# The low part of the weights made by an accumulating DMA instead of a GpSimd subtraction, from the ninth piece on

## The reference

```python
proj = jnp.einsum('bsd,dp->bsp', nx, w_in[l])
...
h = h + jnp.einsum('bsm,md->bsd', mixed, w_out[l])
...
a = jnp.square(jax.nn.relu(jnp.einsum('bsd,df->bsf', nm, w_ff1[l])))
h = h + jnp.einsum('bsf,fd->bsd', a, w_ff2[l])
...
ffn = (jax.nn.silu(hn @ w_gate) * (hn @ w_up)) @ w_down
```

## Time and profile before

| | |
|---|---|
| median of 3 runs | 1548.32 us (1547.88 to 1549.98) |
| the profiled execution: time | 1547.88 us |
| its span | 1546.5 us |
| busy: PE, DVE, ACT, POOL | 94%, 53%, 42%, 36% |
| mean granted TensorE clock | 0.966 of full speed |
| HBM read | 126.93 MB |

### The profile page before, as it was taken

How to read it: one execution, slowest core, us unless ns; L and a number is a source line. 1 busy time by engine, 2 the same in 40 slices (tenths; PEclk the granted TensorE clock), 3 DMA queues, 4 the chain that set the end, 5 groups by cost and what they waited for, 6 DMA issues and landing times.

```text
span 1546.5 us, 17691 instructions
## 1 busy us (share of the span) xinstructions
PE 1449.0 (94%) x6886; PEld 1155.5 (75%) x6886; DVE 824.0 (53%) x1177; ACT 642.1 (42%) x1048; POOL 550.8 (36%) x230
## 2 busy tenths in 40 slices
PE   6989999899999999978988989999899989998998
PEld 4877766688888888856766767787688768876886
DVE  4063466731222313666499889884656642662462
ACT  4353345442322324443466566555344422441340
POOL 3432121344343434333222222223344444444441
PEclk9998899999999999999999999999999999999999
DMA  5321220222222323212211112226232222222321
GB/s 197 117 91 43 66 89 28 82 82 96 96 96 95 98 93 99 92 55 69 68 56 55 55 55 82 81 97 204 83 96 82 96 82 95 95 82 87 104 71 66
DMA packets 41400, 134.39 MB, mean 87 GB/s; under 512 B 4739, under 2 KB 4755, under 8 KB 41189
## 3 DMA queue, kind: packets, MB, share of 16 engines
q1 hardware_dynamic: 40452, 131.67, 26.1%
q10 hardware_dynamic: 864, 1.60, 0.3%
HBM read 126.93 MB, written 6.32 MB: 86 GB/s over the span
## 4 chain that ended last, share of the span: by engine, by line
PE 56%; DVE 27%; ACT 10%; issue 6%; DMA 1%; POOL 0%; DVEq 0%; ACTq 0%; POOLq 0%
PE bank L397 17%; PE bank L399 16%; PE bank L401 16%; DVE ft L1570 4%; DVE ft L1568 3%; ACT WH L689 2%; DVE eb L1306 2%; DVE eb L1302 1%; PE bank L507 1%; DVE ft L1577 1%; ACT AH L980 1%; DVE ft L1563 1%; ACT ft L650 1%; ACT ft L640 1%; ACT ft L638 1%
## 5 line engine op out<-in xcount | busy, mean ns | idle before, releaser
L1629 POOL TENSOR_TENSOR WL<-RAW,WH 128x1024 fp32r<-128x1024 f32 (+2 forms) x225 | 548.3, 2445 | 976.5 <-ACT WH L689 976.1
L397 PE MATMUL bank<-NH,WH 128*128 128x512 f32 x1152 | 475.6, 413 | 12.2 <-ACT NH L670 7.2
L399 PE MATMUL bank<-NL,WH 128*128 128x512 f32 x1152 | 458.3, 398 | 12.7 <-DVE NL L1244 7.7
L401 PE MATMUL bank<-NH,WL 128*128 128x512 f32 x1152 | 456.9, 397 | 0.2 <-POOL WL L1629 0.2
L689 ACT ACTIVATE WH<-RAW 128x1024 fp32r<-128x1024 f32 (+2 forms) x227 | 234.3, 1036 | 298.9 <-PE bank L401 290.2
L397 PEld LDWEIGHTS bank<-NH,WH 128*128 128x128 f32 x1152 | 221.1, 192 | 81.2 <-issue 30.8
L399 PEld LDWEIGHTS bank<-NL,WH 128*128 128x128 f32 x1152 | 221.2, 192 | 63.2 <-DVE NL L1244 9.7
L401 PEld LDWEIGHTS bank<-NH,WL 128*128 128x128 f32 x1152 | 221.0, 192 | 47.9 <-POOL WL L1629 0.6
L397 PE MATMUL bank<-AH,WH 128*128 128x512 f32 x432 | 173.6, 402 | 16.1 <-ACT AH L980 15.7
L1332 DVE TENSOR_TENSOR hT<-hT,bank 128x512 f32<-128x512 f32 x80 | 54.9, 686 | 232.2 <-PE bank L401 232.1
L399 PE MATMUL bank<-AL,WH 128*128 128x512 f32 x432 | 173.1, 401 | 0.0
(11 more groups left out here) (268 smaller groups left out, 1671.2 us busy)
## 6 DMA issues: line engine op xcount, KB each, us to landing
RAW<-in_w_in SPq DMA_DIRECT2D x64, 512.0 KB, 3.8
RAW<-in_w_ff SPq DMA_DIRECT2D x64, 512.0 KB, 3.7
RAW<-in_w_gu SPq DMA_DIRECT2D x44, 512.0 KB, 3.7
RAW<-in_w_down SPq DMA_DIRECT2D x20, 512.0 KB, 3.7
RAW<-in_w_out SPq DMA_DIRECT2D x16, 512.0 KB, 3.8
gates<-hs SPq DMA_DIRECT2D x16, 256.0 KB, 3.3
gw<-gates SPq DMA_DIRECT2D x16, 256.0 KB, 5.9
RAW<-in_w_branch SPq DMA_DIRECT2D x8, 512.0 KB, 3.9
```

The lines of the kernel that those rows point to most:

```text
L397: e.matmul(o, a[0], a[1], start=(k == 0), stop=False)
L399: e.matmul(o, b[0], b[1], start=False, stop=False)
L401: mm = e.matmul(o, c[0], c[1], start=False, stop=(k == t.kt - 1))
L1629: e.tensor_tensor(WL[p % HL][:, 0:n], RAW[p % RAWS][:, 0:n], WH[p % HL][:, 0:n].bitcast(F32), ALU.subtract).then_inc(*pool.sig("low", p))
```

## The change

From the piece with number ADDED = 8 on (219 of 227 pieces), WL isn't subtracted by GpSimd any more. ACT writes the negated high part into WL (a second ACT copy with scale -1), and a DMA that GpSimd issues reads the piece of weights from HBM a second time and adds it into WL, so that WL = W - WH. RAW is now free as soon as WH is made. The negation stands at `split_time(p) + 1.5`, the DMA at `split_time(p) + 3.0`. Each of the five slots has a semaphore of its own for the DMA's end.

```diff
+        ADDED = 8
+
         def low(p):
-            return ("low_first" if p < 2 else "low", p)
+            return ("low_first" if p < 2 else "low" if p < ADDED else f"low_added{p % HL}", p)
...
+        def low_time(p):
+            return split_time(p) + (3.0 if p >= ADDED else 0.05)
...
+            def negated():
+                for p, (u, k, m) in enumerate(plan.pieces):
+                    if p >= ADDED:
+                        yield split_time(p) + 1.5
+                        n = m * plan.units[u][4]
+                        act.wait_ge(("high", p))
+                        e.activation(WL[p % HL][:, 0:n], WH[p % HL][:, 0:n].bitcast(F32), ACT.Copy,
+                                     scale=-1.0).then_inc(*act.sig("high_negated", p))
...
-                    yield split_time(p) + 0.05
-                    n = m * plan.units[u][4]
+                    yield low_time(p)
+                    st, name, i, kt, cols, k0 = plan.units[u]
+                    n = m * cols
+                    if p >= ADDED:
+                        src = A[name] if i is None else A[name][i]
+                        pool.wait_ge(("high_negated", p))
+                        e.dma_start(WL[p % HL][:, 0:n], src[:, k * cols:(k + m) * cols],
+                                    accum_op=ALU.add).then_inc(*pool.sig(f"low_added{p % HL}", p, by=16))
+                        continue
...
-                        sp.wait_ge(low(p - RAWS))
+                        sp.wait_ge(low(p - RAWS) if p - RAWS < ADDED else ("high", p - RAWS))
```

More of the change, by code:

```diff
@@ L981, in swiglu @@
                 return [up(t) if t.i % 2 else gate(t) for t in plan.stage["gu", g]]
-            streams = [prologue(), splits(), root("attn", 14.0), columns("attn", 30.0)]
+            streams = [prologue(), splits(), negated(), root("attn", 14.0), columns("attn", 30.0)]
             streams += [natural("vG", vG, "attn"), natural("vD", vD, "attn")]
```

## The result

Four runs of the changed kernel took 1452.33 to 1453.41 us, median **1452.95 us**. The kernel before, in four runs, took 1549.15 us in the median. The profiled execution, 1452.93 us, has a span of 1451.6 us, 94.9 us less than before.

The account below looks back on a forecast made before the run. PE, busy 94%, was taken as at its peak in f1 and f2, with DVE stopped by POOL's subtraction mattering elsewhere. From 1547.88 us, -18 - 13 - 5 = -36 gave 1512 us; range 1482 to 1645, the forecast's own 1482 to 1544.

Parts of the forecast that it names:

- The rival that the change does nothing: DVE's stops have another cause than POOL's subtraction; gains are lost and negations make it some 1557 us; chance 0.02.
- (c): From 77 to 309 us: 7.5 us of DVE stops in the chain go, negations cost 2.5; net gain 5 us.
- (b): Stick and HGRN2, 735 to 1044 us: 20 us of DVE's excess comes through, negations cost 7; net gain 13 us.
- qS, kS and wo2: Two projections for the stick-breaking attention, ahead of 735 us, and a product behind HGRN2 and the gates: 0 us.
- (a): Handovers from gu to dn: PE's waits for AH, 15.7 us, go, with some lower clock behind them; gain 18 us.
- f1, f2 and the middle of gu: Stretches where PE is at its peak, so nothing off PE can shorten them: 0 us.
- The share of a fifth: In stick and HGRN2, a fifth of 34 us of negations on ACT counted as on the path: 7 us.
- The rival that ACT becomes the bound: Every negation of (b) and (c) on the path: 1562 us; chance 0.10, half of it within no change.
- Two passes: Each added DMA takes 3.2 us of all 16 DMA engines; with a load 4.8 us per piece against PE's 5.52.
- 16.5 of cover: Slot A's time from release to first use, 16.5 us; WL was forecast there after 9 to 12 us.
- the rival of late issues: GpSimd's DMA issues wait for DVE, 0.7 us, at most 2.7; with landing above 9 us, 1644 us; chance 0.03.
- The heavy DMA rivals: DMA engines become the bound: 1634 us at three passes, 1848 at four; chance 0.14 up to three, 0.14 beyond.

Follow-up runs that it names:

- the first two experiments: Changed kernel with GpSimd also subtracting each piece in place in RAW: 1558.54 us; that kernel with three memsets in place of the subtraction: 1461.73 us.
- the copy experiment: Changed kernel in which SP also copies every piece from the ninth on from HBM to a spare place in HBM: 1461.53 us.

## Why the prediction was right in direction and short in size

**The mechanism: right.** DVE's stops beside GpSimd's subtraction were named as what the change takes away, and the first two experiments show it. The rival that the change does nothing falls. The stops were read a little too narrowly: besides operations on two tensors in SBUF, some with one input stood still too, as this line of the kernel before shows (ns min/median/max):

```profile
L629 DVE TENSOR_SCALAR sq<-sq x5: 426/430/2451, 30.9 to 1164.3; 128x512 f32<-128x512 f32 x5
```

What failed is the sum. It left out three quarters of DVE's stops in (c), a third of those in (b) and all those in qS, kS and wo2, and it took PE's busy time as fixed.

**(a), 18 us: right, a little small.** The three handovers gave 23.3. The timeline of the first handover (start us, us, engine, line) answers to the earlier trace rows:

```profile
1172.76 0.61 ACT L657 ACTIVATE ft<-ft 128x512 f32<-128x512 f32 x1
...
1173.41 0.69 DVE L1584 TENSOR_TENSOR ft<-ft,rs 128x512 f32<-128x512 f32 x1 [2.07 <-ACT ft L657]
...
1174.14 0.69 DVE L1586 TENSOR_TENSOR ft<-ft,ft 128x512 f32<-128x512 f32 x1
1174.93 0.69 DVE L1593 TENSOR_TENSOR ft<-bank,ft 128x512 f32<-128x512 f32 x1
...
1175.66 0.63 ACT L996 ACTIVATE AH<-ft 128x512 fp32r<-128x512 f32 x1
```

AH's copy begins as the multiplication with the up tile ends. It begins 2.3 and ends 3.0 us after that tile's last matmul (1173.3 us), where about two and a half were forecast, and PE waits for nothing. Short was what comes on top of the waits, counted at 4 us: it is 7.6 (23.3 less the waits of 15.7). The three handovers gave 9.5, 7.8 and 6.1 us.

**f1, f2 and the middle of gu, 0 us: right** to a tenth of a microsecond. This is what a stretch at PE's full rate looks like in advance, and counting matmuls told it rightly.

**(c), 5 us, against 26.3: the step that failed most.** Only the stops at three places of the chain that ended last were priced, 7.5 us. DVE's busy time in the stretch fell by 30 us, some 2 of them because the later stretch holds three operations fewer. A chain shows one path; a stop beside it, once the path is shortened, can be the next one to hold PE up. And the stretch had a granted clock of 0.93, which wasn't priced at all. Two parts of it, columns as in the earlier trace rows, in the kernel before:

```profile
93.00:136.00 43.00, 38.86 (x167) 28.91 (x166) 23.65 (x32) 16.64 (x30) 11.29 (x5) 0.84 0.14 49
165.00:206.00 41.00, 37.88 (x253) 33.74 (x253) 15.60 (x22) 14.31 (x28) 10.10 (x4) 0.88 0.22 71
```

and about the same work in the changed kernel:

```profile
93.00:126.00 33.00, 32.35 (x164) 24.46 (x163) 18.41 (x32) 20.48 (x35) 3.78 (x5) 1.00 0.59 133
153.00:187.00 34.00, 34.00 (x259) 31.14 (x258) 12.68 (x23) 19.03 (x32) 3.46 (x4) 1.00 0.61 148
```

In the first, 167 matmuls keep PE busy for 38.9 us at 0.84, and 164 for 32.4 us at 1.00: of the 10 us gained 6.5 are busy time, and only the rest are waits. In the second PE was idle for 3.1 of 41 us, yet 7 are gained.

**(b), 13 us, against 28.5 from vS to gs: failed in the same way.** The stops were summed over groups that a reader could pick out and "smaller groups", 30 us; DVE's busy time fell by 46. The granted clock of 0.96 was again not priced, and the sum was then cut from 30 to 20 because PE was busy for 281 of 309 us. That cut was wrong in kind: a PE that is busy at the lower clock isn't at its peak either. The low end of the range doesn't follow from these terms: 19.7 us in (a), 30 in (b) and 7.5 in (c) off 1547.88, with no negation on the path, make 1491, not 1482; the measured time lies under both.

**qS, kS and wo2, 0 us, against 12.3.** They weren't looked at. They lie at the edges of the stretches that were, and DVE's busy time in them fell by 20 us.

The common fault of these steps is that PE's busy time, 37.7 us of the gain, was taken as fixed work. The clock was priced only behind the two longest waits.

**The negations: 9.5 us predicted on the path, 15 to 16 measured.** The share of a fifth was a guess at the middle; the place on ACT turned out to be worth nearly 5 us of it, or 14 against it. The rival that ACT becomes the bound has its mechanism, but not its size. (With half of the negations on the path that rival comes to 1532 by its own terms, 29.5 us in place of 9.5, and not to 1537.)

**The added DMA.** Two passes, 3.2 us, were taken for a piece; 45.9% of 1451.6 us over 219 pieces are 3.04, against 1.57 for a plain load by the prediction's own reckoning (27.1% of 1451.6 us for 131.67 MB, 0.524 MB a piece). The Trainium skill, in Collectives: The Full Stack ("The bandwidth ceiling"), gives half the rate of a plain copy for a reduce-scatter, whose addition in the DMA needs two reads on one ring. That is stated for a transfer between cores; the ratio of 1.94 here agrees with it. The landing was underestimated, 8.6 us against 5.3 to 7:

```profile
RAW<-in_w_ff SPq DMA_DIRECT2D x64, 512.0 KB, 6.0
WL<-in_w_ff POOLq DMA_DIRECT2D x64, 512.0 KB, 8.6
```
```profile
L1648 POOL DMA_DIRECT2D WL<-in_w_ff x64: 862/862/883, 252.9 to 607.0; - x64
L1648 POOL DMA_DIRECT2D WL<-in_w_in x62: 862/862/1569, 45.5 to 966.5; - x62
...
DMA to landing us min/median/max: 4.5/8.5/11.5
```
```profile
L636 DVE TENSOR_SCALAR eb<-eb x8: 426/428/585, 652.9 to 703.6; 128x512 f32<-128x512 f32 x8
```

With copy and negation (1.1 us each) and 0.9 for the issue, WL is there 11 to 12 us after the release, and less than 15 with the slowest landing, inside the 16.5 of cover. Of the 219 issues 216 took 862 to 912 ns. The other three, up to 1569 ns, are among the first, two of them beside GpSimd's own conversion of masks. What the rival of late issues describes is there, but small: the three issues of 905 to 912 ns stand beside a TENSOR_SCALAR of DVE (L636), which took 580 to 585 ns there and 428 in the median. So issues came up to 0.05 us late by it, where the rival had up to 2.7, and PE waited for none. The heavy DMA rivals, 0.28 of the chance, rested on packet times as if they filled an engine, which the copy experiment refutes; they, not the forecast, drew the range up to 1645 us, while nothing in it reached below 1482.

What stays open: stops, waits and lower clock went and came back together in every run here, so how much of the 37.7 us belongs to which wait isn't shown. That the subtraction by itself lowers the clock (theory C in the expectations) is ruled out by the kernel before: in f1 and f2 GpSimd subtracts for 150 of 348 us at a granted clock of 1.00.

## What to carry to other kernels

Where GpSimd reads SBUF in bulk beside a DVE that multiplies tensors in SBUF, look at DVE's durations (minimum against maximum of one line) before looking at who waits for GpSimd: PE had waited 0.2 us for it here, and doing without it gained 96, net of the 16 that the negations cost. Price such a change in each stretch that isn't at PE's peak by two numbers: the whole excess of DVE's time there, and what PE can win at most, its idle time and half its time at 1.2 GHz. In (c) these were some 30 and 18 + 16 = 34 us, and 26 were won; in (b) 46 and 28 + 12 = 40, and some 28 were won, the negations already taken off in both. Work that is moved to an engine in a loop should be placed on it by trial: putting a step of 1 us earlier cost 14 us here, putting it later gained 5.

## What the runs showed of the hardware that was not expected

- Memsets on GpSimd (427 us in all) leave DVE's multiplication of two tensors in SBUF at 0.69 us; a subtraction makes it 2.77 to 3.2 us in the median. A TENSOR_SCALAR of DVE with one input stood still beside both: some 430 ns became up to 2451 beside a subtraction, up to 1149 beside a memset, and some 580 beside the issue of a DMA.
- A DMA share of 1.03 delayed no matmul of f1 and f2, so packet times overlap and aren't a measure of what is left. The packet time for the same additions fell when more was moved (3.04 to 2.75 us a piece), and the rate was 286 GB/s.
- More than a third of the gain, 37.7 of 94.9 us, is PE's busy time for the same matmuls: 105 us of the span stood at 1.2 GHz before, 20 after.
